# New step order around the compress, compressed keys as weights, halves joined by transfers, scores from split q and k

## The reference

```python
h = x @ w_in                                  # 1024 -> pool, conv, q, kc, vc, ks, vs, kw, vw, gates, ...
kc = compress(k_cmp_all, cmp_pe[0], cmp_w[0]) # 32 taps, stride 16: chunk c with the first 16 taps,
vc = compress(v_cmp_all, cmp_pe[1], cmp_w[1]) #   chunk c+1 with the last 16, summed
kc = partial_rope(kc, kc_end)
s_c = q . kc;  p_c = masked_softmax(s_c);  o_c = p_c . vc
o_s = masked_softmax(q . ks) . vs             # selected blocks (all are picked here)
o_w = masked_softmax(q . kw) . vw             # window
y_c = (g0*o_c + g1*o_s + g2*o_w) * silu(az)
x = layer_norm(ALPHA * x + (sum_i sigmoid(g_i) * branch_i @ proj_i) @ w_out)
```

## Time and profile before

| | |
|---|---|
| median of 3 runs | 805.83 us |
| profiled execution | 805.21 us, of it 803.6 us span |
| TensorE matmuls busy | 779.5 us (97%) |
| VectorE busy | 545.4 us (68%) |
| ScalarE busy | 392.9 us (49%) |
| mean granted clock of TensorE | 0.99 |

### The profile page before, as it was taken

One profiled execution on the slowest core, in us unless ns is written; L12 is line 12 of the kernel. 1 busy time (PEld: TensorE's weight loads), 2 busy tenths in 40 slices (PEclk: granted clock), 3 DMA queues, 4 the chain that ended last, 5 costly groups with the idle time before them and its releaser, 6 DMA issues.

```text
span 803.6 us, 16797 instructions
## 1 busy us (share of the span) xinstructions
PE 779.5 (97%) x6314; PEld 723.1 (90%) x6314; DVE 545.4 (68%) x1008; ACT 392.9 (49%) x773; POOL 91.2 (11%) x166
## 2 busy tenths in 40 slices
PE   8999899999999999999999979999999999999995
PEld 7998598888889999999869978888888999999994
DVE  4565378987679675656465675888876876665664
ACT  5443156666465544443345531666656464444423
POOL 2341441000123200000000014410000000000000
PEclk9999999999999999999999998999999999999998
DMA  8988467533777766555437765666338366565621
GB/s 306 284 277 281 125 207 250 206 105 103 239 266 241 244 184 183 178 176 173 131 101 243 253 193 179 211 211 211 104 118 304 121 184 184 184 183 178 176 94 54
DMA packets 41689, 153.62 MB, mean 191 GB/s; under 512 B 6288, under 2 KB 7312, under 8 KB 40976
## 3 DMA queue, kind: packets, MB, share of 16 engines
q1 hardware_dynamic: 33312, 114.24, 45.8%
q0 software_dynamic: 8304, 38.37, 14.0%
HBM read 145.77 MB, written 13.34 MB: 198 GB/s over the span
## 4 chain that ended last, share of the span: by engine, by line
PE 86%; DVE 5%; DMA 3%; ACT 2%; issue 1%; SPq 1%; DVEq 0%; ACTq 0%
PE bank L648 22%; PE bank L649 21%; PE bank L650 21%; DMA ring<-weights_dram 3%; PE bank L859 3%; PE bank L666 3%; PE bank L809 1%; DVE w_lo L1162 1%; PE bank L659 1%; PE bank L815 1%; PE bank L980 1%; PE bank L900 1%; PE bank L989 1%; PE bank L839 1%; PE bank L789 1%
## 5 line engine op out<-in xcount | busy, mean ns | idle before, releaser
L1162 DVE TENSOR_TENSOR w_lo<-ring,w_hi 128x1024 fp32r<-128x1024 f32 x202 | 248.3, 1230 | 152.7 <-ACT w_hi L998 148.8
L648 PE MATMUL bank<-x_hi,w_hi 128*128 128x264 f32 x1208 | 349.5, 289 | 1.7 <-DVE w_lo L1162 1.7
L650 PE MATMUL bank<-x_lo,w_hi 128*128 128x264 f32 x1208 | 342.5, 284 | 0.0
L649 PE MATMUL bank<-x_hi,w_lo 128*128 128x264 f32 x1208 | 342.4, 283 | 0.0
L998 ACT ACTIVATE w_hi<-ring 128x1024 fp32r<-128x1024 f32 x202 | 213.0, 1055 | 69.8 <-PE bank L650 34.3
L648 PEld LDWEIGHTS bank<-x_hi,w_hi 128*128 128x128 f32 x1208 | 227.5, 188 | 5.9 <-issue 3.4
L649 PEld LDWEIGHTS bank<-x_hi,w_lo 128*128 128x128 f32 x1208 | 227.8, 189 | 0.3
L650 PEld LDWEIGHTS bank<-x_lo,w_hi 128*128 128x128 f32 x1208 | 226.8, 188 | 0.0
L648 PE MATMUL bank<-h_rounded,w_hi 128*128 128x264 f32 x352 | 102.2, 290 | 0.0
L649 PE MATMUL bank<-h_rounded,w_lo 128*128 128x264 f32 x352 | 100.2, 285 | 0.0
L1050 ACT ACTIVATE h<-bank 128x264 f32<-128x264 f32 x88 | 34.6, 393 | 105.1 <-PE bank L650 96.5
(11 more groups left out here) (240 smaller groups left out, 947.1 us busy)
## 6 DMA issues: line engine op xcount, KB each, us to landing
ring<-weights_dram SPq DMA_DIRECT2D x208, 512.0 KB, 3.7
cache_a<-kcmp_dram POOLq DMA_DIRECT2D x32, 128.0 KB, 3.6
cache_b<-vcmp_dram POOLq DMA_DIRECT2D x32, 128.0 KB, 3.6
cache_a<-ksel_dram POOLq DMA_DIRECT2D x32, 128.0 KB, 2.7
cache_b<-vsel_dram POOLq DMA_DIRECT2D x32, 128.0 KB, 2.8
cache_a<-kwin_dram POOLq DMA_DIRECT2D x2, 2048.0 KB, 12.6
cache_b<-vwin_dram POOLq DMA_DIRECT2D x2, 2048.0 KB, 9.3
kv_dram<-h POOLq DMA_DIRECT2D x2, 1584.0 KB, 7.6
```

The source lines that it names most:

```text
L648: pe.matmul(out, w_high[:, k0 + k, :], high, start=(k == 0), stop=False)
L649: pe.matmul(out, w_rest[:, k0 + k, :], high, start=False, stop=False)
L650: ins = pe.matmul(out, w_high[:, k0 + k, :], rest, start=False, stop=(k == kn - 1))
L1162: dve.tensor_tensor(w_lo[:, slot % RING], ring[:, slot % RING], w_hi[:, d % HI_RING].bitcast(F32), ALU.subtract).then_inc(w_lo_ready, 1)
```

## The change

1. A table `AFTER_DENSE` replaces the order around the compress: `cmp_k` after dense 17, `cmp_v` and `gates` after dense 20, the filling of q's padding (`q_pad`) after dense 21, `cmp_scores` after 22, `cmp_vrows` and the new `cmp_back` after 23, `cmp_soft` after 24.
2. The halves are joined by two transfers per compress (SP, from `halves` to `other`, partitions exchanged) and additions on DVE. TensorE's part of `cmp_sum` goes.
3. In `cmp_scores` the compressed keys are the weights (32 columns each, eight matmuls of 256 columns that write to four partition groups). ACT copies the result (`cs_t`), and `cmp_back` turns it with four transposes.
4. ACT rounds q and k to float32r (`k_split` once a layer, `q_split` once a q tile), DVE forms the rests, and each of the six score products becomes three float32r matmuls.

```diff
+AFTER_DENSE = {
+    8: [("rope", 0)], 9: [("cmp_swap", 0)], 10: [("rope", 1), ("cmp_swap", 1)], 13: [("v_rows", 0), ("v_rows", 1)],
+    15: [("v_new_in", 0)], 16: [("rope", 2)], 17: [("cmp_k", 0)], 18: [("v_new", 0), ("rope", 3)], 19: [("cmp_sum", 0)],
+    20: [("rope", 4), ("cmp_rope", 0), ("cmp_v", 0), ("gates", 0)], 21: [("rope", 5), ("q_pad", 0)],
+    22: [("cmp_scores", 0), ("k_split", 0), ("cmp_sum", 1)], 23: [("cmp_vrows", 0), ("cmp_back", 0)],
+    24: [("q_split", 0), ("cmp_soft", 0)]}
...
-    order += [("cmp_k", 0), ("gates", 0), ("cmp_v", 0), ("cmp_sum", 0), ("cmp_sum", 1), ("dense", 21),
-              ("cmp_rope", 0), ("cmp_vrows", 0), ("dense", 22), ("cmp_scores", 0), ("dense", 23), ("cmp_soft", 0),
-              ("dense", 24)]
...
+            if u == 0:
+                order.append(("cmp_turn", 0))
+            if g2 == 0 and p + 1 < PAIRS:
+                order.append(("q_split", p + 1))
...
+            def cross(l, which):
+
+                for j in range(1 if l else 2):
+                    wait_emptied(sp, l, ("cmp_k", "cmp_v")[which], 0, j)
+                if l:
+                    wait_emptied(sp, l - 1, ("pre_k", "pre_v")[which], 0)
+                for at in (0, HD):
+                    sp.dma_start(other[HD - at:2 * HD - at, which], halves[at:at + HD, which]
+                                 ).then_inc(other_landed[which], 16)
...
-                        for half in range(2):
-                            for g2 in range(2):
-                                ins = pe.matmul(out[g2 * HD:g2 * HD + HD, 0:10 * GP * NC].rearrange(
-                                    "p (s g c) -> p s g c", g=GP, c=NC), ident[:, half * HD:half * HD + HD],
-                                    halves[:, i, :, g2:4:2, half:half + NC], start=(half == 0), stop=(half == 1))
...
+                        for gp in range(GP):
+                            for r in range(R):
+                                ins = pe.matmul(out[32 * r:32 * r + 32, gp * SEQ:(gp + 1) * SEQ],
+                                                kc_bd[:, gp, :, :].rearrange("p a b -> p (a b)"),
+                                                h[:, Q + gp * R + r, 0:SEQ], start=(gp == 0), stop=(gp == GP - 1),
+                                                skip_group_check=True)
...
+                            q_high, k_high = z_r[rows, Q_HI + i % 2, :], z_r[rows, K_HI:K_HI + 4, :]
+                            q_rest, k_rest = h_r[rows, tile, :], h_r[rows, KS:KS + 4, :]
+                            return ((q_high, k_high), (q_rest, k_high), (q_high, k_rest))[part]
...
+                        pe.wait_ge(k_split, l + 1)
+                        pe.wait_ge(q_split, l * PAIRS + i + 1)
+                        for part in range(3):
+                            ins = early_scores(1, part)
+                            late_scores(0, 0, part)
+                        ins.then_inc(early_odd, 1)
+                        for part in range(3):
+                            late_scores(1, 0, part)
+                            late_scores(0, 1, part)
                         pe.wait_ge(early_odd, l * PAIRS + i + 1)
-                        early_scores(0)
+                        for part in range(3):
+                            late_scores(1, 1, part)
+                            early_scores(0, part)
...
+                            for gp in range(GP):
+                                ins = dve.scalar_tensor_tensor(
+                                    out=all_of[rows, gp, 0:NB + 1, 0:NC], in0=first[rows, i, 0:NB + 1, 2 * gp + g2, 0:NC],
+                                    scalar=bias[rows, i:i + 1], in1=second[rows, i, 0:NB + 1, 2 * gp + g2, 1:CT],
+                                    op0=ALU.add, op1=ALU.add)
```

More of the change, by code:

```diff
@@ L210, in banks_of @@
         return [(PT0, PT1)[i]]
-    if step == "cmp_sum":
-        return [(PT1, SA)[i]]
     if step == "one_scores":
@@ L268 @@
 PARAMS_AT = {SLOT_OF[l, "dense", RING]: l for l in range(DEPTH)}
+CROSS_AFTER = {SLOT_OF[l, step, 0]: (l, n) for l in range(DEPTH) for n, step in enumerate(("cmp_k", "cmp_v"))}
 ROPE_Z = [0, 2, 0, 2, 4, 6]
-VECTOR_STEPS = 95
+VECTOR_STEPS = 94
 def trunk(nc, x_in, weights, params, consts, pages, kcmp, vcmp, ksel, vsel, kwin, vwin,
@@ L492, in _ @@
                     swap(*SWAP_AFTER[before])
+                if before in CROSS_AFTER:
+                    cross(*CROSS_AFTER[before])
                 if n in PARAMS_AT:
@@ L1066, in _ @@
                                                   bank[FILL[l, step, i, j][0]][:, 0:CMP_OWN // KT8], ACT.Copy), step, i, j)
+                    elif step == "cmp_scores":
+                        wait_filled(act, l, step, i)
+                        emptied_by(act.activation(cs_t, bank[SA][:, :], ACT.Copy), step, i)
+                    elif step == "k_split":
+                        act.wait_ge(roped, (l + 1) * len(ROPED))
+                        act.activation(z_r[:, K_HI:K_HI + 4, 0:SEQ], h[:, KS:KS + 4, 0:SEQ], ACT.Copy
+                                       ).then_inc(k_hi_ready, 1)
+                    elif step == "q_split":
+                        if i < 2:
+                            wait_filled(act, l, "cmp_scores", 0)
+                        else:
+                            wait_filled(act, l, "scores", i - 2, 2)
+                        act.activation(z_r[:, Q_HI + i % 2, 0:SEQ], h[:, Q + i, 0:SEQ], ACT.Copy
+                                       ).then_inc(q_hi_ready, 1)
                     elif step == "cmp_soft":
@@ L1227, in _ @@
                         dve.wait_ge(q_pad_ready, l + 1)
+                    if step == "cmp_v":
                         wait_emptied(dve, l, "dense", NG)
@@ L1295, in _ @@
-                        emptied_by(ins, step, i)
-                        if which:
+                        dve.wait_ge(other_landed[i], (l + 1) * 2 * 16)
+                        all_of = vc_all if i else kc_all
+                        for g2 in range(2):
+                            rows = slice(g2 * HD, g2 * HD + HD)
+                            first, second = (other, halves) if g2 else (halves, other)
+                            ins = dve.tensor_tensor(bias[rows, i:i + 1], first[rows, i, NB + 1, g2, 0:1],
+                                                    second[rows, i, NB + 1, g2, 1:2], ALU.add)
@@ new lines, in _ @@
+                        link(ins)
+                        for g2 in range(2):
+                            rows = slice(g2 * HD, g2 * HD + HD)
+                            first, second = (other, halves) if g2 else (halves, other)
+                            for gp in range(GP):
+                                ins = dve.scalar_tensor_tensor(
+                                    out=all_of[rows, gp, 0:NB + 1, 0:NC], in0=first[rows, i, 0:NB + 1, 2 * gp + g2, 0:NC],
+                                    scalar=bias[rows, i:i + 1], in1=second[rows, i, 0:NB + 1, 2 * gp + g2, 1:CT],
+                                    op0=ALU.add, op1=ALU.add)
@@ L1323, in _ @@
                                                    bank[SB][:, 2 * P:4 * P]), step, i)
-                    elif step == "cmp_scores":
+                    elif step == "cmp_back":
                         wait_filled(dve, l, step, i)
```

103 lines of the change are left out of this document (46 added, 57 removed).

## The result

The changed kernel takes 802.34 us (median of 9 runs, 801.07 to 804.0), the kernel before 806.79 us (9 runs on the same chip). The ratio is 0.995 [0.9937, 0.9962]: 4.5 us faster. The forecast was 800.4 us, with 5.4 us to be gained. One execution of experiment 9 took 2664.99 us, far above all others, and no median or ratio here holds it.

A forecast was written before the change was run, and what follows sets the result against it. TensorE, busy 779.5 of 803.6 us, was taken as the bound. From 805.2 us, -20.4 - 3.2 + 13.0 + 2.4 + 2.8 = -5.4 gave 799.8, as a median 800.4 us; 8-in-10 range 789 to 810, the forecast's own 796 to 803.4.

The forecast's parts named there:

- a, b: TensorE at the compress: waits at `gates` go, 8.1 us, and the slow half-clock work behind them, 3.7 us.
- c, d: TensorE at the compress, both layers: `cmp_sum`'s records go, 4.4 us; `cmp_scores` gets shorter, 4.2 us.
- The scores step: Each of 16 scores steps on TensorE takes 1.3 us instead of 1.50, 3.2 us less in all.
- Waits before cmp_vrows and scores 0: New TensorE waits for DVE in both layers: 1.6 us before `cmp_vrows`, 3.1 us before `scores 0`.
- The lag behind scores 0: After `scores 0`, DVE's maxima start later: the wait at L839 grows 1.2 us a layer, 2.4 us.
- Before `cmp_rope` in layer 1: TensorE waits for the key halves before `cmp_rope`: 0.5 us, up to 1.7 if the transfer is slow.
- `gates` of layer 1: TensorE waits 3.1 us at `gates` in layer 1 for DVE's rotations and `gate_d`; layer 0 is covered.
- The clock: Low clock behind the three new 3.1 us waits: half of them charged, 2.8 us; bounds 0 and 5.5.
- the first: Rival: DVE keeps up, so waits before `cmp_vrows` and `scores 0` and the lag mostly go; 787.6 us, chance 0.13.
- The second: Rival: the halves don't overlap in the scores step, nine pairs take 2.0 us; 811.6 us, slower, chance 0.13.
- The third: Rival: all three waits bring the low clock and the transfers come late; 804.3 us, no measurable change, chance 0.14.

The follow-up runs named there:

- experiment 9: Changed kernel with reordered compress steps, plain float32 scores for the first two head pairs and split scores for the other six: 792.61 us, ratio 0.9848 to the kernel before.
- Experiment 5: Changed kernel with the score records of one 64-row half in blocks instead of alternating with the other half: 813.81 us, ratio 1.0099 to the kernel before.
- experiments 1: Changed kernel with the value halves added on DVE before k is split: 798.9 us, ratio 0.991 to the kernel before.
- experiment 3: Changed kernel with plain float32 scores, without the splitting of q and k: 796.52 us, ratio 0.9885 to the kernel before.
- experiments 4: Changed kernel with the first q tile split one step earlier, before `cmp_vrows`: 800.27 us, ratio 0.9932 to the kernel before.
- 2: Changed kernel with the `gates` step one dense tile later, after dense 21: 800.19 us, ratio 0.9922 to the kernel before.
- experiment 6: Changed kernel with six unused float32 matmuls added in the wait before `scores 0`: 801.06 us, ratio 0.9941 to the kernel before.
- 7: Changed kernel, split scores kept, with `gates` later, value halves first, `cmp_vrows` behind the turn and q rests moved: 791.05 us, ratio 0.9818 to the kernel before.
- 8: Changed kernel with plain float32 scores, `gates` later, value halves first and `cmp_vrows` behind the turn: 789.19 us, ratio 0.9805 to the kernel before.

## Why the prediction was right, and where it was not

The sign holds, and so does the main mechanism: most of what goes from TensorE's path comes back as waits for DVE and at the low clock. The size of the sum owes something to luck, as the last points show. By its steps:

- **Waits at gates and the half clock behind them** (a, b: 11.8 us). Right. None is left in layer 0, and `cmp_v` of layer 1 runs in 1.95 us.
- **cmp_sum and cmp_scores** (c, d: 8.6 us). Right: the sums are off TensorE, and the compressed scores take 1.07 us for 1.0 forecast.
- **The scores step**, 1.3 forecast, 1.26 measured, and 11.07 - 10.84 = 0.23 us a pair for 0.2. The doubt between 1.3 and 2.0 was settled by the present pairs' overlap, and rightly. Experiment 5 shows that it takes the alternation of the halves.
- **Waits before cmp_vrows and scores 0**, 1.6 and 3.1 forecast; 1.84 and 3.05 in layer 0, 1.83 and 3.13 in layer 1. Right, and experiments 1, 3 and 4 show that DVE's queue makes them: each goes when the instruction in front of it is moved or left out.
- **The lag behind scores 0: mis-sized.** 1.2 us a layer more forecast. The wait for the probabilities there was 0.94 and 0.89 us (L839) and is 1.29 and 1.26 (L862): 0.4 us a layer more. The way from the mask of scores 0 to that of scores 2 did grow by more, from 20.61 to 21.13 us in layer 0 and from 20.55 to 21.96 in layer 1, with two shorter steps in it (0.5), but most of that is the low clock, which lasts 1.6 us into it in layer 0 and 3.4 us in layer 1.
- **Before `cmp_rope` in layer 1: the term that was most wrong among the waits.** Forecast 0.5 us, with 1.7 if the transfer of the halves is slow; measured 1.92. The forecast set the three dense tiles, 8.9 us, against the transfer and left it there. By the trace `cmp_k` ends at 465.0 us, but SP, which has the four small transfers of a `rope` and a weight in front, issues the two transfers only from 467.33 us on:

```profile
467.33 2.46 SPq L492 DMA_DIRECT2D h<-h  x2
```

The second lands at 473.94 us, just when TensorE has got to the wait, and the additions on DVE (1.6 us) are covered by nothing. The transfers themselves weren't slow, at 4.8 and 5.3 us from issue to landing. A second chain ends at the same time: the halves stand on DVE behind a weight's rest, and this weight lands late too. ACT first, then DVE, of the changed kernel:

```profile
471.82 1.06 ACT L1021 ACTIVATE w_hi<-ring 128x1024 fp32r<-128x1024 f32 x1 [3.49 <-DMA ring<-weights_dram]
```
```profile
472.98 1.23 DVE L1199 TENSOR_TENSOR w_lo<-ring,w_hi 128x1024 fp32r<-128x1024 f32 x1 [2.23 <-ACT w_hi L1021]
474.13 0.32 DVE L1326 TENSOR_TENSOR bias<-h 64x1 f32<-64x1 f32 x2
```

ACT waits 3.49 us for the weight, DVE 2.23 us for ACT, and the halves start only behind it, 0.2 us after their own landing. With the weight in time the wait would, by these numbers, still have been some 1.7 us, which is an estimate. In layer 1 of experiments 3, 4 and 9 the transfer came last; DVE of experiment 3:

```profile
471.54 0.32 DVE L1312 TENSOR_TENSOR bias<-h 64x1 f32<-64x1 f32 x2 [0.36 <-DMA h<-h]
```

In all ten profiles with the transfers TensorE waits 1.4 to 3.0 us here. The kernel before shows the same late weight, but had no use for DVE here:

```profile
473.25 1.06 ACT L998 ACTIVATE w_hi<-ring 128x1024 fp32r<-128x1024 f32 x1 [3.71 <-DMA ring<-weights_dram]
```

So the weight's part could have been read from the trace of before: DVE's idle time there ended with that weight.
- **`gates` of layer 1**, 3.1 forecast, 2.13 + 1.27 = 3.4 measured: the transposes wait until DVE has read the bank of the rotated keys (L1349), the matmul for `gate_d`, and both are the one chain that was counted. The 0.3 us more come from 0.87 us in which DVE waited for ACT in it.
- **The clock: mis-sized too.** It was charged 2.8 us, half of what one stretch costs for each of three waits. In the profile all three brought the low clock. TensorE was busy at half clock for 3.4 us in layer 0 and for 6.7 + 3.4 us in layer 1, and half of that, 6.7 us, is lost.

In sum, for the two profiled executions: 20.4 + 3.7 us go, and waits of 15.2 us (13.0 forecast), 0.7 us of lag (2.4) and 6.7 us at the low clock (2.8) come back. That leaves 1.5 us, and the spans differ by 1.2. For layer 1 alone it is +2.0 in waits, +3.2 in the clock and -0.8 in the lag, 4.4 us more than forecast, against the 4.2 by which its stretch missed. In layer 0 clock and lag were off by 0.8 us each, in opposite directions, which is why that stretch came out as forecast.

So the forecast hit the medians (4.5 us gained, 5.4 forecast) more closely than it hit the terms, and that is luck in part. It is not shown why the medians lie 4.5 us apart and these two executions 1.3: the mean clock of the profiled executions, 0.990 and 0.988, lies amid that of the other runs of the same kernels (0.988 to 0.992 and 0.985 to 0.990). The low clock itself differs from profile to profile. In layer 1 it lasts 10.2 us in the changed kernel and in experiments 4 and 5, and 6.8 us in experiments 1, 2 and 6, of which 1 has it in both places, 2 behind `scores 0` alone and 6 at `gates` alone.

Of the rivals, the first (DVE keeps up) was wrong as the change stands, since the chains held no slack; but the orders of 7 and 8, with 791.05 and 789.19 us, come near the 787.6 us that it named, so much of that time was in the order. The second needs another order of the records. The third, all three waits with the low clock and a late transfer, is what the profile shows: 6.7 us at the low clock for the rival's 5.5, and 1.92 us before `cmp_rope` for its 1.7. Its 804.3 us is close to the profiled execution's 804.0; the median of 802.34 us lies in the forecast's range.

## What to carry to other kernels

Where work goes from the busiest engine to one that is idle for a third of the time, ask where the receiving engine's own queue is full just then: the first user of the new result waits behind everything that stands in front of it, and a local chain against what the busy engine does meanwhile priced five of these waits within 0.3 us. The one that it missed hung on a transfer and a weight that landed together and late, so a chain must begin with what its engine itself waits for at that point, and a transfer's chain with the queue that issues it. Removing a single wait gave 1 to 3 us, since the next step collected the debt; moving the whole group gave 11. And before a faster form of an operation is kept, undo it alone: here it cost some 5 us as placed, and brought no gain that could be measured even when well placed.

## What the runs showed of the hardware that was not expected

- Float32r records on 64 rows with their own weight loads run side by side, a pair each 0.12 us, if the two halves alternate in the queue. In a block of one half each takes the 0.12 us by itself (1.97 us a step instead of 1.26). A partner three places further on was still run beside (experiment 5).
- Plain float32 records with 32-column weights that write to four partition groups run side by side as well. The 16 of the compressed scores start in four sets of four, at 96.76, 97.00, 97.22 and 97.43 us, those of a set within 0.02 us. That is what the 0.06 us each of the earlier trace rows was made of.
- An idle time of 1.84 us before `cmp_vrows` was followed by 3.4 us at the low clock in layer 0 of experiment 6, and by none in the changed kernel and in experiment 5, with the same code up to there. Which idle time brings the low clock was not the same in each execution.
- A wait can differ between executions by more than many a change is worth. The one before `cmp_rope` in layer 0 was between 0 and 1.4 us in ten profiles that run the same instructions up to it.
